# Expert blocks: the transposes of the hidden tile stand inside the next block's gate and up products

## The reference

```python
def run_block(args):
    xb, e = args
    hid = jax.nn.silu(xb @ w_gate[e]) * (xb @ w_up[e])
    return hid @ w_down[e]

yb = lax.map(run_block, (buf.reshape(n_blocks, MOE_BLOCK, D), block_e)).reshape(n_rows, D)
y = jnp.zeros((T, D), jnp.float32).at[tok_s].add(yb[dest].astype(jnp.float32) * w_s[:, None])
```

## Time and profile before

| what | value |
|---|---|
| median of 3 runs | 3573.23 us (3568.24 to 3577.52) |
| span of the profiled execution | 3572.6 us |
| PE busy | 3425.6 us, 96% of the span |
| DVE busy | 1974.0 us, 55% |
| ACT busy | 1559.2 us, 44% |
| matmuls | 23462 |
| mean granted TensorE clock, share of full | 0.981 |
| moved by DMA | 488.14 MB, mean 137 GB/s |

### The profile page before, as it was taken

How to read it: one execution, slowest core, us unless ns; L and a number is a source line. 1 busy time by engine, 2 the same in 40 slices (tenths; PEclk the granted TensorE clock), 3 DMA queues, 4 the chain that set the end, 5 groups by cost and what they waited for, 6 DMA issues and landing times. The chain is left out here.

```text
span 3572.6 us, 54793 instructions
## 1 busy us (share of the span) xinstructions
PE 3425.6 (96%) x23462; PEld 2748.2 (77%) x23462; DVE 1974.0 (55%) x2532; ACT 1559.2 (44%) x1820; POOL 180.4 (5%) x179
## 2 busy tenths in 40 slices
PE   7999999989999999799999999999999999999998
PEld 5787676776666666587888888888788887888886
DVE  4544444455555555457556775355656657663444
ACT  4322110345555554344355664444433457654533
POOL 0000000000000000100010000000000011000000
PEclk9899999999999999899999999999999999999999
DMA  5100343358999998412110111053222111011333
GB/s 206 48 27 36 120 157 122 122 202 320 373 368 372 366 371 328 178 48 89 60 61 31 60 72 54 26 205 130 77 71 83 49 61 49 28 75 48 142 123 106
DMA packets 95913, 488.14 MB, mean 137 GB/s; under 512 B 10752, under 2 KB 11264, under 8 KB 57776
## 3 DMA queue, kind: packets, MB, share of 16 engines
q1 hardware_dynamic: 77216, 417.31, 31.6%
q0 software_dynamic: 12688, 46.27, 3.6%
q10 hardware_dynamic: 5760, 20.97, 1.4%
HBM read 427.23 MB, written 57.28 MB: 136 GB/s over the span
## 5 line engine op out<-in xcount | busy, mean ns | idle before, releaser
L136 PE MATMUL ps<-HH,WS 128*128 128x512 f32 (+1 forms) x2608 | 1046.4, 401 | 11.9 <-DVE WS L1387 9.4
L138 PE MATMUL ps<-HH,WS 128*128 128x512 f32 (+1 forms) x2608 | 1022.5, 392 | 0.0
L137 PE MATMUL ps<-HL,WS 128*128 128x512 f32 (+1 forms) x1968 | 772.1, 392 | 0.0
L136 PEld LDWEIGHTS ps<-HH,WS 128*128 128x128 f32 (+1 forms) x2608 | 493.2, 189 | 126.2 <-DVE WS L1387 12.5
L138 PEld LDWEIGHTS ps<-HH,WS 128*128 128x128 f32 (+1 forms) x2608 | 492.2, 189 | 107.6
L1450 ACT ACTIVATE WA<-ps 128x512 f32<-128x512 f32 x240 | 142.4, 594 | 801.5 <-PE ps L138 708.0
L137 PEld LDWEIGHTS ps<-HL,WS 128*128 128x128 f32 (+1 forms) x1968 | 372.5, 189 | 75.2 <-issue 1.0
L1387 DVE TENSOR_TENSOR WS<-RAW,WS 128x1024 fp32r<-128x1024 f32 (+1 forms) x153 | 200.7, 1313 | 161.1 <-ACT WS L1382 161.1
L136 PE MATMUL ps<-WS,HH 128*128 128x256 f32 x896 | 262.8, 293 | 13.4 <-DVE HL L2315 12.2
L137 PE MATMUL ps<-WS,HH 128*128 128x256 f32 x896 | 255.7, 285 | 0.0
L138 PE MATMUL ps<-WS,HL 128*128 128x256 f32 x896 | 255.6, 285 | 0.0
(11 more groups left out here) (413 smaller groups left out, 5197.5 us busy)
## 6 DMA issues: line engine op xcount, KB each, us to landing
WR<-in_weu SPq DMA_DIRECT2D x37, 1024.0 KB
WR<-in_weg SPq DMA_DIRECT2D x35, 1024.0 KB
WR<-in_wed SPq DMA_DIRECT2D x34, 1024.0 KB
RAW<-in_wo SPq DMA_DIRECT2D x32, 1024.0 KB, 4.9
H<-in_wed SPq DMA_DIRECT2D x26, 1024.0 KB, 9.0
WA<-in_wada SPq DMA_DIRECT2D x48, 512.0 KB
H<-in_weg SPq DMA_DIRECT2D x23, 1024.0 KB, 7.8
H<-in_weu SPq DMA_DIRECT2D x21, 1024.0 KB, 7.1
```

The costliest lines, as they stand in the source:

```text
L136: t.matmul(o, l[0], r[0], start=st, stop=False)
L137: t.matmul(o, l[0], r[1], start=False, stop=False)
L138: return t.matmul(o, l[1], r[0], start=False, stop=sp)
```

## The change

TensorE's `turn(j-1)` is called from within `hidden(j)`, behind k = 3, so that its four transposes stand between the 24th and the 25th of the 48 matmuls. VectorE's copy of them is the first instruction of its round, ahead of the rests of pieces 0 and 1. Nothing is added or removed, and the plan of banks and buffers is the same.

```diff
-            def hidden(j):
+            def hidden(j, between=None):
...
                     if k == 3:
                         o.then_inc(*up("gu_half", j))
+                        if between is not None:
+                            turn(between)
                 o.then_inc(*up("gu_mm", j))
...
             start(0)
             for j in range(FIRST + 1):
                 if j < FIRST:
-                    hidden(j)
-                if j:
+                    hidden(j, j - 1 if j else None)
+                else:
                     turn(j - 1)
                 if j + 1 < FIRST:
                     start(j + 1)
...
             bounds_vector(v, 2)
             start(0)
             for j in range(FIRST + 1):
+                if j:
+                    turn(j - 1)
                 if j + 1 < FIRST:
                     vector_expert_split(v, j + 1, 0)
                     vector_expert_split(v, j + 1, 1)
-                if j:
-                    turn(j - 1)
                 if j < FIRST:
                     gate(j)
```

## The result

| | before | changed |
|---|---|---|
| median | 3572.11 us (3568.24 to 3577.52, 4 runs) | 3550.11 us (3549.6 to 3554.3, 4 runs) |
| ratio | | 0.9936, 95% interval 0.9923 to 0.9949 |
| span of the profiled execution | 3572.6 us | 3552.5 us |

The changed kernel is 22 us faster; 3548.0 was forecast, 3542 to 3556 the range. Its profiled execution is the slowest of its four runs (3554.3 us, 1.8 above its span); the other three have spans of 3547.8 to 3548.3. Only the slowest one has a trace; what the clock does between executions is read from it further down.

What follows compares the result with a forecast made beforehand. TensorE was taken to bound the experts' stretch. 30 x 0.82 + 1.22 - 30 x 0.02 = 25.2 us off the 3572.6 us span gave 3547.4, so a median of 3548.0 us; range 3542 to 3556.

Steps and rivals of the forecast that it cites:

- What the wait was made of: TensorE idle before the first down matmul L981 for VectorE's copy: 0.74 us late in round 10, 0.46 queue, 0.28 latency.
- The removed wait: Last L942 to second L981 on TensorE: 1.36 us falls to 0.54, gaining 0.82 us in each of 30 rounds.
- the slow first L981: First down matmul took 0.51 us instead of 0.43; if not due to the wait, the gain is 0.74 us a round.
- The cost of the cut: Extra change from 512-column matmuls to transposes and back within hidden: 0.02 us a round taken, bounded by 0 and 0.08.
- round 31: Round without rests or L942 between transposes and L981: 1.76 us to the second L981 becomes 0.54, gaining 1.22 us.
- What hides the copy: VectorE's copy fits in 0.8 us before the rests can start; without that cover the rests still end 7 us early.
- Does it reach the end: Links behind PE's last L981 each start from the one before, so the whole tail shifts and the span drops 25.2 us.
- The DMA rival: DMA engines become the bound in the experts' stretch at 369 GB/s: 3563 us, or 3573 without slack; chance 0.05.
- The gather's slack: Gather of block 12 lands 9.3 us before its reader; at 0.8 us a round this lasts 11 or 12 rounds.
- The clock rival: Transposes in two places lower TensorE's clock for part of each round; 3.2 us a round would give 3596 us; chance 0.03.

Runs made afterwards that it cites:

- VectorE's half alone: Against the kernel before: only VectorE's copy moved to the head of its round, transposes left behind the 48th matmul; 3562.56 us, ratio 0.9971.
- TensorE's half alone: Against the kernel before: only the four transposes moved to the middle of hidden, VectorE's copy left behind the rests; 3576.91 us, ratio 1.0004.
- the second series: Later timings beside the kernel before (3576.58 us), including the changed kernel again without edit: 3546.62 us, ratio 0.9918.
- The run with two products: Against the changed kernel: third product (rest of the activations by rounded weights) left out, hidden cut from 48 to 32 matmuls; 3486.94 us.

## Why the prediction was right, point by point

*What the wait was made of.* The working put 0.46 us of it to the rests queued ahead of the copy and 0.28 to bare latency. VectorE's half alone moved L981 by 0.46 and left 0.28; TensorE's half alone gave nothing, since the queue still set the copy's start. Both are shown.

*The removed wait.* From the last L942 to the second L981 1.36 us stood against a forecast of 0.54. Measured after: 0.54, so the slow first L981 (0.51 us) belonged to the wait, and the higher of the two values, 0.82, was right.

*The cost of the cut.* This term was mis-sized: 0.02 us a round was taken, 0.04 to 0.05 measured at the cut. In the first trace of the changed kernel another 0.03 came at the head of the round, which makes 0.08, the prediction's upper bound. The return itself costs what the earlier trace rows show: in the changed kernel the last transpose starts at 999.93 and the L137 at 1000.26 (0.335 us with more digits). What the earlier trace rows end too soon to show is the stretch behind it: from 1000.26 to 1002.35 nine matmuls take 2.09 us, from 1002.35 to 1004.39 the next nine 2.04. Over 30 rounds the error was about 1.8 us, and it is what separates rounds of 19.16 from the 19.10 forecast. The prediction's sum, 25.2, became 30 x 0.74 + 1.15 = 23.4 by the median round (23.6 by the rounds themselves), where round 31 gave 1.15 of the 1.22 expected.

*What hides the copy.* 0.8 us of cover was forecast and 0.82 measured. The statement that no cover is needed holds too: with VectorE's half alone the rests of pieces 0 and 1 ended 4.6 us later in the round and nothing waited for them.

*Does it reach the end.* To L442 yes, 23.4 us. In the profiled execution 3.3 us were lost behind it, mostly through the clock of later layers, and the range had a few us for that. In the second series the same program was 30 us ahead of the kernel before, in the result 22. By the rounds the stage is worth 23 to 25 (30 x 0.74 or 0.78, and 1.15; the kernel before was traced only once, so its 19.90 is taken for both). The rest of the 30 was not traced to a place. With medians of one program that lie 3.5 us apart (3550.11 and 3546.62), a time within 2.1 us of the forecast is in part luck; the rounds and the two halves carry the proof, not the time.

*The DMA rival.* It had 0.05, on the ground that 426 GB/s had been seen for 2 us. The run with two products settles it: 422 GB/s over 300 us can be had, and the changed kernel draws 383. The gather's slack was not used up either, since PE has no wait for it in the stretch. The limit of about 358 GB/s that the Trainium skill gives (DMA: Bandwidth & Descriptors, "Where 436 GB/s comes from") is a memory stack's bandwidth divided by two cores; with one core at work all three figures, 369, 383 and 422, exceed it.

*The clock rival.* The granted clock stayed at 1.00 through the stretch, with TensorE's transposes in two places. It is refuted for this stage. Its price was read loosely: three of the eight matmuls of the earlier trace rows are float32 ones (L1635); that the others take twice as long holds, for from 3378.12 us on they stand 0.43 us apart, against 0.227 at the upper level. What the clock does elsewhere was larger than the few us that the prediction allowed: two executions of the changed kernel have spans that lie 8.3 us apart, of which the rounds explain 1.2 us. That is more than a third of the gain, and more than what tells the versions of the changed kernel from each other.

## What to carry to other kernels

A wait of the bounding engine for another engine can be two things, as it was here, a queue there and the latency of the hand-over; read both from the trace (a round in which nothing is queued ahead shows the latency alone), because each is mended at another engine, and mending the latency was worth nothing here as long as the queue stood ahead of it. Put the hand-over as early as its input allows, behind enough work of the bounding engine, and put its partner early enough in its queue: early enough is a number that a timeline gives, and being first isn't needed. When versions differ by less than the clock's chance elsewhere, compare the length of a round in the trace and not the time.

## What the runs showed of the hardware

- In the changed kernel, some of the 512-column matmuls right behind the four float32 transposes, and right behind the float32 matmuls at the round's head, stand 0.231 to 0.232 us apart on average instead of 0.227, with no wait in the profile. The same program differs between executions: nine distances at either place in the first trace (19.16 us a round); two at the head and five in the middle in the second (19.12); the same in all rounds of an execution. At the head the kernel before has it too, for two distances, so it doesn't come from transposes alone. The cause stays open.
- The first float32 matmul of 512 columns starts 0.50 us ahead of its successor when it had to wait (before, and in each half alone), and 0.43 us when it follows a transpose without a wait (the changed kernel).
- 16 DMA engines moved 422 GB/s for 300 us with one core at work, and the profile gives their busy share as 1.01. At a share of 0.97, with 369 GB/s, they were still 13% under that, so a share near 1 was no proof that they bind.
